# Merged tiles split into high and low parts inside the merging stage, whose block begins the output projection's first two tiles

## Chip, cores and metric

The kernel runs on one NeuronCore of a Trainium2 chip. The metric is the device time of one execution in microseconds (us); of the kernel before it is the median of three runs.

## The reference, cut to what matters

A block of four branches (RWKV-7, latent attention, convolution, memory attention) is run for two layers, and after it a second, different block. The change is in the end of each layer of the first block:

```
h = x @ w_in[l]                                   # x: 512 x 1024; merge: the last 4*1024 columns
branches = stack([y_rwkv, y_mla, y_conv, y_mem])  # 512 x 4 x 512
proj   = einsum('bsnc,ncd->bsnd', branches, w_o_branch[l])
gates  = sigmoid(merge.reshape(B, S, 4, D) + b_gate[l])
merged = sum(gates * proj, axis=2)                # 512 x 1024
out    = merged @ w_out[l]
x      = layer_norm(alpha * x + out)
```

Beside it the second block needs a modulation: silu(cond) (two rows of 1024) times a matrix w_ada of 1024 x 6144 in each of its two layers.

## The kernel before

Everything is kept transposed: a tile is 128 channels (partitions) by 512 positions, fp32, and a tensor of 1024 channels is eight tiles. A product of fp32 precision is made from three fp32r products: each operand is split into a high part (rounded by ScalarE's copy to fp32r) and a low part (what is left, by a subtraction). One output tile takes 24 matmuls: 8 of high weight x high data, 8 of high weight x low data (helper `with_high`, lines 155 and 158), 8 of low weight x high data.

**Weights** come as a stream of chunks of 512 KB (`Stream`, from line 93), each one a tile's weights of 1024 columns. SyncE sends chunk n into one of three ring slots, after the low part of chunk n-3 is made. ScalarE makes the high part (line 123) into one of two slots, after TensorE has begun the chunk before (count `used`), GpSimd makes the low part (line 131). All queues work strictly in the order written.

**The merging stage** of a layer is one block. A block ends on every engine when the slowest engine is done. It has 48 chunks, here counted 0 to 47. Step i (0 to 31) belongs to merged tile m = i // 4 and branch n = i % 4. TensorE takes them in pairs: the gate products of two steps (one chunk each, PSUM bank i % 4), then one chunk which holds w_o of both branches (PSUM banks 4 + n). So chunks 3p and 3p+1 are the gates of pair p and chunk 3p+2 is its projection. ScalarE takes the sigmoid of gate i (line 1669). VectorE first makes the low parts of the sixteen branch tiles (line 1682, count `branch_low`), then in step i multiplies product and gate (line 1690) and adds it to the merged tile in BR (line 1695).

**The modulation** is done by VectorE within the same steps (line 1703): w_ada comes as 48 rows of tiles ("rows", 512 KB each), and each row is multiplied and summed with the two conditions, two instructions a row. Row t is done in step i where 48 i // 30 <= t < 48 (i+1) // 30. SyncE issues rows and ring chunks from one queue, in turns: ahead of row t it sends the ring up to chunk 2 + 45 t // 48. Row t goes into one of four buffers, so row t (t >= 4) is issued when row t-4 is done (line 1630); rows 2 and 3 wait until the branch tiles that they overwrite are split (`branch_low` 12 and 16). The two conditions are loaded at the very start. After the last step a copy (line 1705) puts the modulation into `mods`.

**The output stage** (function `output`, line 1717) is the next block. ScalarE makes the high parts of the eight merged tiles and VectorE their low parts, and TensorE's tile t = 0 follows these k by k; tiles 1 to 7 have all eight. GpSimd goes on with low parts of weights. Then the residual is added. In layer 1 this block also loads parameters, constants and the context tile `ctxT` of the second block (`Context.sync`, lines 1896 to 1899), the last of these after `merged_low` 4, as it overwrites the merged tiles in BR, and normalises the context beside the products. SyncE begins a block by clearing 47 semaphores.

Of the kernel before, what the change touches and what calls it, by code (L numbers as in the profile page):

```python
# [174 lines left out]
def build(nc, A):  # L175
    with ExitStack() as ctx:
# [32 lines left out]
        with ExitStack() as one:  # L209
            first(nc, one, A, PS, XH, XL, BR, stream, mods, stage, loaded)  # L210
        with ExitStack() as two:
            second(nc, two, A, PS, XH, XL, BR, stream, mods, stage, constants, stored)
# [271 lines left out]
def first(nc, ctx, A, PS, XH, XL, BR, stream, mods, stage, loaded):  # L484
# [169 lines left out]
    for layer in range(LAYERS):  # L654
# [945 lines left out]
        Y = room.enter_context(nc.sbuf_tensor(f"merging{layer}", [P, 18 * T], F32))  # L1600

        def YT(i, n=1):
            return Y[:, i * T:(i + n) * T] if n == 1 else Y[:, i * T:(i + n) * T].rearrange("p (n t) -> p n t", n=n)

        GATE, WEIGHTED, MG = YT(0, 4), YT(4, 4), BR[:, 0:8, :]
        AD = WEIGHTED[:, 0, 0:96].rearrange("p (m c) -> p m c", c=2)
        PROD, CB = Y[:, 8 * T:10 * T], Y[:, 10 * T:14 * T].rearrange("p (c k) -> p c k", c=2)

# [3 lines left out]
        def rows_of(t):  # L1612
            s = t % 4
            return Y[:, (14 + 2 * s) * T:(16 + 2 * s) * T] if s < 2 else BR[:, 4 + 2 * s:6 + 2 * s, :].rearrange("p a t -> p (a t)")

        S, other = stage()
        with nc.Block() as block:
            @block.sync
            def _(sp):
                for c in range(2):  # L1620
                    sp.dma_start(CB[:, c, :], A["cond"][c].partition_broadcast(P)).then_inc(S("cond"), 16)
                stream.send(sp, n0 + RING)
                clear(sp, other)
                for t in range(48):
                    stream.send(sp, n0 + RING + 45 * t // 48)
                    if t >= 4:
                        sp.wait_ge(S("ada"), 2 * (t - 3))
                    elif t >= 2:
                        sp.wait_ge(S("branch_low"), 4 + 4 * t)
                    sp.dma_start(rows_of(t), A["ada"][layer, t, :, :]).then_inc(S(f"rows{t % 4}"), 16)  # L1630
                stream.send(sp, n0 + 48 + RING - 1)

            @block.tensor
            def _(pe):
                for m in range(8):
                    for n in (0, 2):
# [15 lines left out]
                        for nn in (n, n + 1):  # L1652
                            for k in range(4):
                                mm = nc.tensor.matmul(PS[:, 4 + nn, :], tile_of(stream.low(o), 4 * (nn % 2) + k), BH[:, 4 * nn + k, :], start=False, stop=(k == 3))
                            mm.then_inc(S("product"), 1)

            @block.scalar
            def _(act):
                def branch_high(b):
                    nc.scalar.activation(BH[:, b, :], BR[:, b, :], ACT.Copy).then_inc(S("branch_high"), 1)  # L1660

                stream.hi(nc, act, gate_chunk(1) + 1)
                for b in range(8):
                    branch_high(b)
                for i in range(32):
                    act.wait_ge(S("gate_product"), i + 1)
                    if i >= 4:
                        act.wait_ge(S("weighted"), i - 3)
                    nc.scalar.activation(GATE[:, i % 4, :], PS[:, i % 4, :], ACT.Sigmoid, bias=par_col("b_gate", 8 * (i % 4) + i // 4)).then_inc(S("gate"), 1)  # L1669
                    stream.hi(nc, act, min(gate_chunk(i) + (4 if i % 2 else 3), n0 + 48 + 1))  # L1670
                    if i == 0:
                        for b in range(8, 16):
                            branch_high(b)
                        act.wait_ge(S("cond"), 32)
                        nc.scalar.activation(CB, CB, ACT.Silu).then_inc(S("silu_c"), 1)

            @block.vector
            def _(dve):
# [4 lines left out]
                for i in range(32):  # L1683
# [3 lines left out]
                    dst = MG[:, m, :] if n == 0 else WEIGHTED[:, n, :]  # L1687
                    if i >= 4 and n:
                        dve.wait_ge(S("merged"), 3 * m - 3 + n)
                    v.tensor_tensor(dst, PS[:, 4 + i % 4, :], GATE[:, i % 4, :], ALU.mult).then_inc(S("weighted"), 1)  # L1690
                    if n:
                        dve.wait_ge(S("weighted"), i + 1)
                        if n > 1:
                            dve.wait_ge(S("merged"), 3 * m + n - 1)
                        v.tensor_tensor(MG[:, m, :], MG[:, m, :], WEIGHTED[:, n, :], ALU.add).then_inc(S("merged"), 1)
                    if i == 0:
                        dve.wait_ge(S("silu_c"), 1)
                    for t in range(min(48, 48 * i // 30), min(48, 48 * (i + 1) // 30)):
                        dve.wait_ge(S(f"rows{t % 4}"), 16 * (t // 4 + 1))
# [4 lines left out]
                dve.wait_ge(S("ada"), 96)  # L1704
                v.tensor_copy(mods[:, layer, :], WEIGHTED[:, 0, 0:96]).then_inc(S("mods"), 1)
# [7 lines left out]
        if layer == 0:  # L1713
            output(nc, PS, XH, XL, BR, stream, stage, base + FIRST["out"], layer, oneless[:, 0:1], C("ones"))


def output(nc, PS, XH, XL, BR, stream, stage, n0, layer, spare, ones, context=None):
# [4 lines left out]
    room = ExitStack()  # L1722
    MH, ML = (room.enter_context(nc.sbuf_tensor(f"merged_{part}{layer}", [P, DK, T], F32R))[:, :, :] for part in ("high", "low"))
    MG, RR, RUN = BR[:, 0:8, :], BR[:, 8:16, :], BR[:, 7, :]
    S, other = stage()
    with nc.Block() as block:
# [13 lines left out]
        def _(pe):  # L1740
            for t in range(8):
                if t >= 4:
                    pe.wait_ge(S("residual"), t - 3)
                if t == 0:
                    stream.wait_high(pe, n0)
                    for k in range(DK):
                        pe.wait_ge(S("merged_low"), k + 1)
                        with_high(nc, PS[:, 0, :], tile_of(stream.high(n0), k), MH[:, k, :], ML[:, k, :], k == 0, stream.used if k == 0 else None)
                    stream.wait_split(pe, n0)
                    for k in range(DK):  # L1750
                        mm = nc.tensor.matmul(PS[:, 0, :], tile_of(stream.low(n0), k), MH[:, k, :], start=False, stop=(k == DK - 1))
# [13 lines left out]
        def _(act):  # L1765
            a = nc.scalar
            for k in range(DK):
# [17 lines left out]
        def _(dve):  # L1785
            v = nc.vector
            for k in range(DK):
                dve.wait_ge(S("merged_high"), k + 1)
                v.tensor_tensor(ML[:, k, :], MG[:, k, :], MH[:, k, :].bitcast(F32), ALU.subtract).then_inc(S("merged_low"), 1)
            for t in range(8):  # L1790
# [4 lines left out]
                if t:  # L1795
# [3 lines left out]
                    if t == 1:  # L1799
                        dve.wait_ge(S("merged_low"), 8)  # L1800
# [3 lines left out]
    room.close()  # L1804
# [36 lines left out]
def second(nc, ctx, A, PS, XH, XL, BR, stream, mods, stage, constants, stored):  # L1841
# [44 lines left out]
    class Context:  # L1886
# [139 lines left out]
    for layer in range(LAYERS):  # L2026
# [7 lines left out]
        if layer == 0:  # L2034
            context = Context(mixed)
            output(nc, PS, XH, XL, BR, stream, stage, (LAYERS - 1) * NCHUNK1 + FIRST["out"], LAYERS - 1, spare[:, 0:1], C("ones"), context)
# [977 lines left out]
```

## Time and profile before

| | us |
|---|---|
| median of three runs | 3420.7 (3420.3 to 3421.48) |
| the profiled execution, its time | 3420.07 |
| its span, first to last instruction | 3418.3 |
| TensorE busy | 3225.6, 94% of the span |
| merging stage, layer 0, about | 597 to 868 |
| output stage, layer 0, about | 868 to 923 |

The span is what the profiler sees between the first and the last instruction; 1.8 us lie around it. Busy matmul time overlaps from one matmul to the next, so the distance from start to start is what a matmul costs. SPq is SyncE's DMA queue: a row of it is the time of issue, not of landing. The bracket at the end of a timeline row gives how long the engine was idle ahead of it and who released it.

### The profile page before, as it was taken

What the parts mean: (1) busy time and instruction counts of PE and PEld (TensorE: products, weight loads), DVE (VectorE), ACT (ScalarE), POOL (GpSimd) and SP (SyncE); (2) the same over time, 40 slices, a digit from 0 to 9 for tenths busy, and PEclk for the clock granted to TensorE, in tenths of its full rate; (3) what the DMA queues carried; (4) which work ended last, traced back from release to release, by engine and by line L of the source; (5) the groups of instructions that cost most, each with busy time, mean ns of one, the idle gap of its engine ahead of it and who ended that gap; (6) DMA issues with size and microseconds to landing.
All of it is one profiled execution on the core that took longest, in us unless ns stands there. A gap on an engine that the chain in (4) does not pass through costs nothing. (4 is left out here: it accounts for less than half of the span.)

```text
span 3418.3 us, 51762 instructions
## 1 busy us (share of the span) xinstructions
PE 3225.6 (94%) x21116; PEld 2532.1 (74%) x21116; DVE 1500.7 (44%) x2378; ACT 1188.0 (35%) x1940; POOL 1488.2 (44%) x820
## 2 busy tenths in 40 slices
PE   8899998999898999989998988999999989899999
PEld 6784786788577747867886756888888876678787
DVE  6633374898666333848896236210000022520000
ACT  6234433422362334343223435322112233532221
POOL 4431553454344225534552258333334433845454
PEclk9999999999999999999999999999999999999999
DMA  3011121555210111325552210212111111023232
GB/s 127 9 34 55 56 99 62 209 191 200 76 62 3 39 55 51 106 86 189 200 185 85 87 32 2 68 62 62 62 62 62 62 60 56 1 87 99 93 99 93
DMA packets 77611, 284.18 MB, mean 83 GB/s; under 512 B 8736, under 2 KB 8736, under 8 KB 76864
## 3 DMA queue, kind: packets, MB, share of 16 engines
q1 hardware_dynamic: 77376, 280.88, 24.4%
q8 instruction: 168, 2.75, 0.3%
q14 instruction: 67, 0.55, 0.1%
HBM read 278.75 MB, written 2.10 MB: 82 GB/s over the span
## 5 line engine op out<-in xcount | busy, mean ns | idle before, releaser
L131 POOL TENSOR_TENSOR lows<-ring,highs 128x1024 fp32r<-128x1024 f32 x376 | 939.1, 2498 | 1607.3 <-ACT highs L123 1590.4
L155 PE MATMUL ps<-x_high,highs 128*128 128x512 f32 x1936 | 771.6, 399 | 36.2 <-ACT highs L123 17.4
L158 PE MATMUL ps<-x_low,highs 128*128 128x512 f32 x1936 | 758.7, 392 | 0.0
L123 ACT ACTIVATE highs<-ring 128x1024 fp32r<-128x1024 f32 x376 | 396.9, 1056 | 749.9 <-PE ps L155 388.4
L155 PEld LDWEIGHTS ps<-x_high,highs 128*128 128x128 f32 x1936 | 366.2, 189 | 127.1 <-issue 30.7
L158 PEld LDWEIGHTS ps<-x_low,highs 128*128 128x128 f32 x1936 | 365.9, 189 | 78.3 <-issue 3.5
L2744 DVE TENSOR_TENSOR hidden_scratch<-ps,hidden_scratch 128x512 f32<-128x512 f32 x44 | 30.4, 692 | 546.0 <-PE ps L2063 541.5
L677 PE MATMUL ps<-x_high,lows 128*128 128x512 f32 x1040 | 256.8, 389 | 0.0
L677 PEld LDWEIGHTS ps<-x_high,lows 128*128 128x128 f32 x1040 | 195.3, 188 | 40.5
L2620 DVE SCALAR_TENSOR_TENSOR BR<-ps,mod,BR 128x512 f32<-128x512 f32 x72 | 47.4, 662 | 368.8 <-PE ps L167 368.8
L167 PE MATMUL ps<-hidden_parts,lows 128*128 128x512 f32 (+1 forms) x528 | 188.8, 358 | 0.0
L163 PE MATMUL ps<-hidden_parts,highs 128*128 128x512 f32 (+1 forms) x528 | 188.8, 358 | 0.0
L166 PE MATMUL ps<-hidden_parts,highs 128*128 128x512 f32 (+1 forms) x528 | 188.8, 358 | 0.0
L1703 DVE CUSTOM_DVE_ANT_0 merging<-merging 128x1024 f32<-128x1024 f32 x96 | 174.8, 1821 | 3.4
L2063 PE MATMUL ps<-x_high,lows 128*128 128x512 f32 x672 | 167.1, 391 | 0.0
L1703 DVE CUSTOM_DVE_ANT_0 merging<-BR,merging 128x1024 f32<-128x1024 f32 x96 | 164.3, 1711 | 5.5 <-DVE merging L1703 0.5
L428 POOL TENSOR_SCALAR tiles<-tiles 128x768 f32<-128x768 f32 (+1 forms) x80 | 154.9, 1948 | 25.5 <-DVE tiles L453 25.5
L1558 DVE SCALAR_TENSOR_TENSOR ps<-X,par,ps 128x512 f32<-128x512 f32 x232 | 152.9, 750 | 0.0
L2063 PEld LDWEIGHTS ps<-x_high,lows 128*128 128x128 f32 x672 | 123.3, 188 | 24.0
L428 POOL TENSOR_SCALAR X<-X 128x256 f32<-128x256 f32 (+3 forms) x96 | 97.7, 1032 | 67.2 <-DVE X L453 67.1
L1669 ACT ACTIVATE merging<-ps,par 128x512 f32<-128x512 f32 x64 | 44.1, 690 | 232.7 <-PE ps L677 232.7
L447 DVE TENSOR_REDUCE tiles<-ps 128x1 f32<-128x768 f32 (+1 forms) x80 | 67.7, 846 | 106.4 <-PE ps L330 106.2
(435 smaller groups left out, 5917.5 us busy)
## 6 DMA issues: line engine op xcount, KB each, us to landing
ring<-in_w SPq DMA_DIRECT2D x414, 512.0 KB, 3.5
merging<-in_ada SPq DMA_DIRECT2D x48, 512.0 KB, 3.5
BR<-in_ada SPq DMA_DIRECT2D x48, 512.0 KB, 3.5
X<-in_xT SPq DMA_DIRECT2D x4, 512.0 KB, 6.7
X<-in_memT SPq DMA_DIRECT2D x2, 1024.0 KB, 5.3
merging<-in_cond SPq DMA_DIRECT2D x4, 512.0 KB, 4.7
out<-BR SPq DMA_DIRECT2D x8, 256.0 KB, 4.4
cst<-in_cst SPq DMA_DIRECT2D x1, 1408.0 KB, 7.7
```

The lines of the kernel that those rows point to most:

```text
L123: nc.scalar.activation(self.high(n), self.chunk(n), ACT.Copy).then_inc(self.hi_made, 1)
L131: nc.gpsimd.tensor_tensor(self.low(n), self.chunk(n), self.high(n).bitcast(F32), ALU.subtract).then_inc(self.lo_made, 1)
L155: mm = nc.tensor.matmul(ps, high, xhigh, start=start, stop=False)
L158: nc.tensor.matmul(ps, high, xlow, start=False, stop=False)
L163: mm = nc.tensor.matmul(ps, high, xhigh, start=start, stop=False)
L166: nc.tensor.matmul(ps, high, xlow, start=False, stop=False)
L167: return nc.tensor.matmul(ps, low, xhigh, start=False, stop=stop)
L428: nc.gpsimd.tensor_scalar(prob(i, u), prob(i, u), stats[:, 3, n:n + 1], None, ALU.mult).then_inc(S("normed"), 1)
L677: mm = nc.tensor.matmul(PS[:, bank, :], tile_of(stream.low(n), k), xh[:, k, :], start=False, stop=(k == DK - 1))
L1558: ins = v.scalar_tensor_tensor(out=ACC[:, c, :] if tap == TAPS - 1 else acc, in0=H0[:, c, tap:tap + T], scalar=w, in1=acc, op0=ALU.mult, o ...
L1703: v.tensor_tensor_reduce(PROD, rows_of(t), CB[:, c, :], 1.0, 0.0, ALU.mult, ALU.add, AD[:, t, c:c + 1]).then_inc(S("ada"), 1)
L2063: mm = nc.tensor.matmul(ps, tile_of(stream.low(n), k), high[:, k, :], start=False, stop=(k == DK - 1))
```

## The change

- The merged tile is accumulated in one of two buffers in BR (tiles 8 and 9) instead of eight. In step i = 4m (m >= 1) ScalarE makes the high part of merged tile m-1, in step 4m+1 VectorE makes its low part, into tiles MH and ML that outlive the merging block. Only tile 7 is split in the output block.
- At the end of the merging block TensorE does the high-weight products of output tiles 0 and 1 for k = 0 to 6 (28 matmuls). The output block does k = 7 of each and its 8 low-weight products. ScalarE makes one more high part (chunk 49) in the merging block.
- Buffers: the gates have three buffers instead of four, the weighted product one instead of three, and both lie in BR with the conditions, the product scratch and two of the rows. So they wait for `branch_low`. The rows have three buffers instead of four: row t waits for row t-3. Row 0 has its own buffer; row 1 waits for `branch_low` 14, row 2 for 16; the conditions are loaded after `branch_low` 4, and SyncE clears the semaphores ahead of that.
- Row t is done in the step with 48 i // 29 <= t < 48 (i+1) // 29. The modulation is summed directly in `mods`; the copy at the end is gone. The wait of the context's load for `merged_low` 4 is gone.

```diff
-        Y = room.enter_context(nc.sbuf_tensor(f"merging{layer}", [P, 18 * T], F32))
-
-        def YT(i, n=1):
-            return Y[:, i * T:(i + n) * T] if n == 1 else Y[:, i * T:(i + n) * T].rearrange("p (n t) -> p n t", n=n)
-
-        GATE, WEIGHTED, MG = YT(0, 4), YT(4, 4), BR[:, 0:8, :]
-        AD = WEIGHTED[:, 0, 0:96].rearrange("p (m c) -> p m c", c=2)
-        PROD, CB = Y[:, 8 * T:10 * T], Y[:, 10 * T:14 * T].rearrange("p (c k) -> p c k", c=2)
+        Y = room.enter_context(nc.sbuf_tensor(f"merging{layer}", [P, 2 * T], F32))
+        kept = ExitStack()
+        MH, ML = (kept.enter_context(nc.sbuf_tensor(f"merged_{part}{layer}", [P, DK, T], F32R, side="right"))[:, :, :] for part in ("high", "low"))
+
+        def flat(a, n):
+            return BR[:, a:a + n, :].rearrange("p a t -> p (a t)")
+
+        CB, GATE, WEIGHTED = flat(0, 4).rearrange("p (c k) -> p c k", c=2), BR[:, 4:7, :], BR[:, 7, :]
+        MG, PROD = BR[:, 8:10, :], flat(10, 2)
+        AD = mods[:, layer, :].rearrange("p (m c) -> p m c", c=2)
+        ROWS = (Y[:, :], flat(12, 2), flat(14, 2))
...
+            return ROWS[t % 3]
 
         S, other = stage()
         with nc.Block() as block:
             @block.sync
             def _(sp):
+                stream.send(sp, n0 + RING)
+                clear(sp, other)
+                sp.dma_start(rows_of(0), A["ada"][layer, 0, :, :]).then_inc(S("rows0"), 16)
+                sp.wait_ge(S("branch_low"), 4)
                 for c in range(2):
                     sp.dma_start(CB[:, c, :], A["cond"][c].partition_broadcast(P)).then_inc(S("cond"), 16)
-                stream.send(sp, n0 + RING)
-                clear(sp, other)
-                for t in range(48):
+                for t in range(1, 48):
                     stream.send(sp, n0 + RING + 45 * t // 48)
-                    if t >= 4:
-                        sp.wait_ge(S("ada"), 2 * (t - 3))
-                    elif t >= 2:
-                        sp.wait_ge(S("branch_low"), 4 + 4 * t)
-                    sp.dma_start(rows_of(t), A["ada"][layer, t, :, :]).then_inc(S(f"rows{t % 4}"), 16)
+                    if t < 3:
+                        sp.wait_ge(S("branch_low"), 12 + 2 * t)
+                    else:
+                        sp.wait_ge(S("ada"), 2 * (t - 2))
+                    sp.dma_start(rows_of(t), A["ada"][layer, t, :, :]).then_inc(S(f"rows{t % 3}"), 16)
                 stream.send(sp, n0 + 48 + RING - 1)
...
+                for t in range(2):
+                    pe.wait_ge(S("gate"), 29 + t)
+                    stream.wait_high(pe, n0 + 48 + t)
+                    for k in range(7):
+                        pe.wait_ge(S("merged_low"), k + 1)
+                        with_high(nc, PS[:, t, :], tile_of(stream.high(n0 + 48 + t), k), MH[:, k, :], ML[:, k, :], k == 0, used if t == 0 and k == 0 else None)
...
-                    if i >= 4:
-                        act.wait_ge(S("weighted"), i - 3)
-                    nc.scalar.activation(GATE[:, i % 4, :], PS[:, i % 4, :], ACT.Sigmoid, bias=par_col("b_gate", 8 * (i % 4) + i // 4)).then_inc(S("gate"), 1)
+                    if i >= 3:
+                        act.wait_ge(S("weighted"), i - 2)
+                    else:
+                        act.wait_ge(S("branch_low"), 5 + i)
+                    nc.scalar.activation(GATE[:, i % 3, :], PS[:, i % 4, :], ACT.Sigmoid, bias=par_col("b_gate", 8 * (i % 4) + i // 4)).then_inc(S("gate"), 1)
                     stream.hi(nc, act, min(gate_chunk(i) + (4 if i % 2 else 3), n0 + 48 + 1))
+                    if i >= 4 and i % 4 == 0:
+                        act.wait_ge(S("merged"), 3 * i // 4)
+                        nc.scalar.activation(MH[:, i // 4 - 1, :], MG[:, (i // 4 - 1) % 2, :], ACT.Copy).then_inc(S("merged_high"), 1)
                     if i == 0:
                         for b in range(8, 16):
                             branch_high(b)
                         act.wait_ge(S("cond"), 32)
                         nc.scalar.activation(CB, CB, ACT.Silu).then_inc(S("silu_c"), 1)
+                stream.hi(nc, act, n0 + 48 + 2)
...
-                    dst = MG[:, m, :] if n == 0 else WEIGHTED[:, n, :]
-                    if i >= 4 and n:
-                        dve.wait_ge(S("merged"), 3 * m - 3 + n)
-                    v.tensor_tensor(dst, PS[:, 4 + i % 4, :], GATE[:, i % 4, :], ALU.mult).then_inc(S("weighted"), 1)
+                    if i == 0:
+                        dve.wait_ge(S("branch_low"), 16)
+                    if n:
+                        dve.wait_ge(S("merged"), 3 * m + n - 1)
+                    v.tensor_tensor(WEIGHTED if n else MG[:, m % 2, :], PS[:, 4 + i % 4, :], GATE[:, i % 3, :], ALU.mult).then_inc(S("weighted"), 1)
                     if n:
                         dve.wait_ge(S("weighted"), i + 1)
-                        if n > 1:
-                            dve.wait_ge(S("merged"), 3 * m + n - 1)
-                        v.tensor_tensor(MG[:, m, :], MG[:, m, :], WEIGHTED[:, n, :], ALU.add).then_inc(S("merged"), 1)
+                        v.tensor_tensor(MG[:, m % 2, :], MG[:, m % 2, :], WEIGHTED, ALU.add).then_inc(S("merged"), 1)
                     if i == 0:
                         dve.wait_ge(S("silu_c"), 1)
-                    for t in range(min(48, 48 * i // 30), min(48, 48 * (i + 1) // 30)):
-                        dve.wait_ge(S(f"rows{t % 4}"), 16 * (t // 4 + 1))
+                    if i >= 5 and n == 1:
+                        dve.wait_ge(S("merged_high"), m)
+                        v.tensor_tensor(ML[:, m - 1, :], MG[:, (m - 1) % 2, :], MH[:, m - 1, :].bitcast(F32), ALU.subtract).then_inc(S("merged_low"), 1)
+                    for t in range(min(48, 48 * i // 29), min(48, 48 * (i + 1) // 29)):
+                        dve.wait_ge(S(f"rows{t % 3}"), 16 * (t // 3 + 1))
                         for c in range(2):
                             if 2 * t + c:
                                 dve.wait_ge(S("ada"), 2 * t + c)
                             v.tensor_tensor_reduce(PROD, rows_of(t), CB[:, c, :], 1.0, 0.0, ALU.mult, ALU.add, AD[:, t, c:c + 1]).then_inc(S("ada"), 1)
-                dve.wait_ge(S("ada"), 96)
-                v.tensor_copy(mods[:, layer, :], WEIGHTED[:, 0, 0:96]).then_inc(S("mods"), 1)
...
-                if t == 0:
-                    stream.wait_high(pe, n0)
+                if t < 2:
+                    pe.wait_ge(S("merged_low"), 1)
+                    with_high(nc, PS[:, t, :], tile_of(stream.high(n0 + t), 7), MH[:, 7, :], ML[:, 7, :], False, stream.used if t else None)
+                    stream.wait_split(pe, n0 + t)
                     for k in range(DK):
-                        pe.wait_ge(S("merged_low"), k + 1)
-                        with_high(nc, PS[:, 0, :], tile_of(stream.high(n0), k), MH[:, k, :], ML[:, k, :], k == 0, stream.used if k == 0 else None)
-                    stream.wait_split(pe, n0)
-                    for k in range(DK):
-                        mm = nc.tensor.matmul(PS[:, 0, :], tile_of(stream.low(n0), k), MH[:, k, :], start=False, stop=(k == DK - 1))
+                        mm = nc.tensor.matmul(PS[:, t, :], tile_of(stream.low(n0 + t), k), MH[:, k, :], start=False, stop=(k == DK - 1))
...
-                a.activation(MH[:, k, :], MG[:, k, :], ACT.Copy).then_inc(S("merged_high"), 1)
-                if k == 1:
-                    stream.hi(nc, act, n0 + 2)
+            a.activation(MH[:, 7, :], BR[:, 9, :], ACT.Copy).then_inc(S("merged_high"), 1)
...
+            dve.wait_ge(S("merged_high"), 1)
+            v.tensor_tensor(ML[:, 7, :], BR[:, 9, :], MH[:, 7, :].bitcast(F32), ALU.subtract).then_inc(S("merged_low"), 1)
...
-            sp.wait_ge(S("merged_low"), 4)
             sp.dma_start(cT.rearrange("p k t -> p (k t)"), A["ctxT"]).then_inc(S("c_in"), 16)
```

## Rows read from the trace of the kernel before

**Rows 1.** The page's first part: busy us of each engine, its share, instructions.

```profile
PE 3225.6 (94%) x21116; PEld 2532.1 (74%) x21116; DVE 1500.7 (44%) x2378; ACT 1188.0 (35%) x1940; POOL 1488.2 (44%) x820
```

**Rows 2.** Busy by stretch: PE, PEld, DVE, ACT, POOL; clock, DMA, GB/s.

```profile
620.00:700.00 80.00, 80.00 (x350) 65.41 (x349) 66.63 (x75) 20.78 (x25) 38.39 (x15) 1.00 0.52 184
...
868.00:885.00 17.00, 12.25 (x40) 9.31 (x41) 8.15 (x11) 6.39 (x10) 4.35 (x2) 0.70 0.28 93
```

**Rows 3.** Timeline, end of merging, layer 0: start, us, engine, line, what.

```profile
862.33 2.03 PE L1654 MATMUL ps<-branches_high,lows 128*128 128x512 f32 x8
...
867.84 0.20 DVE L1705 COPY mods<-merging 128x96 f32<-128x96 f32 x1
...
868.34 1.15 ACT L1768 ACTIVATE merged_high<-BR 128x512 fp32r<-128x512 f32 x2 [7.92 <-PEq L1617]
...
869.85 0.76 PE L155 MATMUL ps<-merged_high,highs 128*128 128x512 f32 x1 [5.49 <-DVE merged_low L1789]
...
874.79 0.80 PE L155 MATMUL ps<-merged_high,highs 128*128 128x512 f32 x1 [2.90 <-DVE merged_low L1789]
...
881.36 0.40 PE L155 MATMUL ps<-merged_high,highs 128*128 128x512 f32 x1
...
886.96 0.40 PE L155 MATMUL ps<-merged_high,highs 128*128 128x512 f32 x1
```

**Rows 4.** Timeline of TensorE at the same place of layer 1.

```profile
1794.29 2.03 PE L1654 MATMUL ps<-branches_high,lows 128*128 128x512 f32 x8
...
1813.29 0.40 PE L155 MATMUL ps<-merged_high,highs 128*128 128x512 f32 x1
```

**Rows 5.** Timeline of SyncE's queue, start of merging, layer 0.

```profile
602.16 0.43 SPq L112 DMA_DIRECT2D ring<-in_w  x1
...
610.60 0.33 SPq L1630 DMA_DIRECT2D BR<-in_ada  x1
...
613.01 0.33 SPq L1630 DMA_DIRECT2D BR<-in_ada  x1
```

**Rows 6.** Timeline, ScalarE and TensorE: high of chunk 3, its use.

```profile
615.02 1.05 ACT L123 ACTIVATE highs<-ring 128x1024 fp32r<-128x1024 f32 x1
...
616.12 0.50 PE L155 MATMUL ps<-x_high,highs 128*128 128x512 f32 x1 [2.05 <-ACT highs L123]
```

**Rows 7.** Timeline of SyncE's queue: ring chunks 10, 19 and 33 before.

```profile
644.17 0.43 SPq L112 DMA_DIRECT2D ring<-in_w  x1
...
695.48 0.43 SPq L112 DMA_DIRECT2D ring<-in_w  x1
...
773.27 0.43 SPq L112 DMA_DIRECT2D ring<-in_w  x1
```

**Rows 8.** Timeline: TensorE's first of chunks 9, 18, 33; ScalarE's high of 19.

```profile
649.27 0.40 PE L155 MATMUL ps<-x_high,highs 128*128 128x512 f32 x1
...
698.87 0.40 PE L155 MATMUL ps<-x_high,highs 128*128 128x512 f32 x1
...
699.95 1.06 ACT L123 ACTIVATE highs<-ring 128x1024 fp32r<-128x1024 f32 x1 [4.35 <-DMA ring<-in_w]
...
781.53 0.40 PE L155 MATMUL ps<-x_high,highs 128*128 128x512 f32 x1
```

**Rows 9.** Stretch 600 to 868: low parts by form; line 1695, min/median/max ns.

```profile
L131 POOL TENSOR_TENSOR lows<-ring,highs 128x1024 fp32r<-128x1024 f32 x48 | 131.7, 2745 | 137.6 <-ACT highs L123 137.6
...
L1695 DVE TENSOR_TENSOR BR<-BR,merging x24: 691/695/2670, 617.0 to 867.2; 128x512 f32<-128x512 f32 x24
```

**Rows 10.** Timeline of TensorE after a wait elsewhere in the kernel.

```profile
2135.41 0.77 PE L163 MATMUL ps<-mixed_parts,highs 128*128 128x512 f32 x1 [2.49 <-DVE mixed_parts L2616]
...
2138.43 0.40 PE L166 MATMUL ps<-mixed_parts,highs 128*128 128x512 f32 x1
```

**Rows 11.** Output stage, layer 1: SyncE's first load; the context's DMA.

```profile
1803.71 0.33 SPq L1896 DMA_DIRECT2D par<-in_par  x1
...
BR<-in_ctxT SPq DMA_DIRECT2D x1, 1024.0 KB, 4.8
```

More of the change, by code:

```diff
@@ L209, in build @@
         with ExitStack() as one:
-            first(nc, one, A, PS, XH, XL, BR, stream, mods, stage, loaded)
+            merged = first(nc, one, A, PS, XH, XL, BR, stream, mods, stage, loaded)
         with ExitStack() as two:
-            second(nc, two, A, PS, XH, XL, BR, stream, mods, stage, constants, stored)
+            second(nc, two, A, PS, XH, XL, BR, stream, mods, stage, constants, stored, merged)
 def clear(sp, sems, done=None):
@@ L1612, in rows_of @@
         def rows_of(t):
-            s = t % 4
-            return Y[:, (14 + 2 * s) * T:(16 + 2 * s) * T] if s < 2 else BR[:, 4 + 2 * s:6 + 2 * s, :].rearrange("p a t -> p (a t)")
+            return ROWS[t % 3]
         S, other = stage()
@@ L1713, in first, with output @@
         if layer == 0:
[L1714 to L1724, printed above, removed]
+            output(nc, PS, XH, XL, BR, stream, stage, base + FIRST["out"], layer, oneless[:, 0:1], C("ones"), (kept, MH, ML))
+    return kept, MH, ML
+def output(nc, PS, XH, XL, BR, stream, stage, n0, layer, spare, ones, merged, context=None):
+    kept, MH, ML = merged
+    RR, RUN = BR[:, 8:16, :], BR[:, 7, :]
     S, other = stage()
@@ L1766, in _ @@
             a = nc.scalar
-            for k in range(DK):
-                a.activation(MH[:, k, :], MG[:, k, :], ACT.Copy).then_inc(S("merged_high"), 1)
-                if k == 1:
-                    stream.hi(nc, act, n0 + 2)
+            a.activation(MH[:, 7, :], BR[:, 9, :], ACT.Copy).then_inc(S("merged_high"), 1)
             for t in range(3, 10):
@@ L1786, in _ @@
             v = nc.vector
-            for k in range(DK):
-                dve.wait_ge(S("merged_high"), k + 1)
-                v.tensor_tensor(ML[:, k, :], MG[:, k, :], MH[:, k, :].bitcast(F32), ALU.subtract).then_inc(S("merged_low"), 1)
+            dve.wait_ge(S("merged_high"), 1)
+            v.tensor_tensor(ML[:, 7, :], BR[:, 9, :], MH[:, 7, :].bitcast(F32), ALU.subtract).then_inc(S("merged_low"), 1)
             for t in range(8):
@@ L1798, in _ @@
                         dve.wait_ge(S("run"), t - 1)
-                    if t == 1:
-                        dve.wait_ge(S("merged_low"), 8)
                     v.tensor_tensor(RUN, RR[:, 0, :] if t == 1 else RUN, RR[:, t, :], ALU.add).then_inc(S("run"), 1)
@@ L1803, in _ @@
                     context.vector(dve, S, t)
-    room.close()
+    kept.close()
 CKV = CTX + T
@@ L1838, with second @@
 NCHUNKS = _at
-def second(nc, ctx, A, PS, XH, XL, BR, stream, mods, stage, constants, stored):
+def second(nc, ctx, A, PS, XH, XL, BR, stream, mods, stage, constants, stored, merged):
     def sb(name, shape, dt=F32):
@@ L2035, in second @@
             context = Context(mixed)
-            output(nc, PS, XH, XL, BR, stream, stage, (LAYERS - 1) * NCHUNK1 + FIRST["out"], LAYERS - 1, spare[:, 0:1], C("ones"), context)
+            output(nc, PS, XH, XL, BR, stream, stage, (LAYERS - 1) * NCHUNK1 + FIRST["out"], LAYERS - 1, spare[:, 0:1], C("ones"), merged, context)
         lower = ExitStack()
```

## The prediction

> **What bounds the kernel now.** The page's first part comes first: the reader sees TensorE busy for 94% of the span and every other engine below half [rows 1]. So the time is TensorE's instructions plus what it waits, and a change which removes no matmul can only gain or lose waits. The stretches tell where they are: inside the merging stage TensorE has no idle time (80.00 of 80.00) at a granted clock of 1.00, while VectorE is busy for 66.63 of 80 us; from 868 to 885 TensorE is busy for 12.25 of 17.00 us, and the clock is 0.70, partly at its lower level of 1.2 GHz [rows 2]. The timeline of that place shows why: the last projection matmuls of merging start at 862.33, VectorE ends with the modulation's copy at 868.04, ScalarE's first high part starts 0.30 us later, and TensorE's first matmul of the output at 869.85, after 5.49 us of idleness; a second wait of 2.90 us follows at 874.79 [rows 3]. Layer 1 repeats it: 19.00 us from its last group to the first matmul of output tile 1, against 19.03 in layer 0 [rows 3, 4]. Last I read SyncE's queue in merging, since the change shortens its lookahead [rows 5, 7].
>
> **The junction: what goes.** I count from Z, the start of the last group of eight projection matmuls. Matmuls at full clock start (886.96 - 881.36) / 24 = 0.233 us apart. Before, output tile 2 starts at Z + 24.63 (886.96 - 862.33) in layer 0 and at Z + 19.00 + 5.60 = Z + 24.60 in layer 1. After, the group of eight takes 1.87, then 28 matmuls 6.53, and the last is done at about Z + 8.56. VectorE is no longer the last to end the block: it ended at Z + 5.71 with the copy of 0.20, and its rows now end one step sooner, so TensorE ends it. The low part of merged tile 6 is made in step 29, before the last products are out, and covers nothing more. Then 0.30 for the next block and 1.51 (868.34 to 869.85) for high and low part of tile 7: TensorE goes on at Z + 10.37. Twenty matmuls (k = 7 twice for each of two tiles, eight low ones for each) take 4.67: tile 2 starts at Z + 15.04. That is 9.59 us less in layer 0 and 9.56 in layer 1, **19.15 in all**. The idle time there falls to 1.8 us. What is late next is ScalarE's high part of chunk 50: it waits for tile 1's first matmul of this block, ten matmuls after Z + 10.37, so it is made by about Z + 14.2, under a microsecond ahead of tile 2.
>
> **The clock at the junction.** A wait of 2.05 us left the following matmuls 0.4 us long [rows 6]; one of 2.49 was followed by 0.77, and seven start-to-start distances took 3.02 us where full clock needs 1.63 [rows 10]. 1.8 us is below the first, so I take nothing; if it falls after all, it costs 1.4 a layer. I keep 0 to 2.8 for the range.
>
> **The start of merging: chunk 3.** Ring and rows share one queue, in order. Before, chunk 3 was sent at 602.16, ahead of row 2's wait. After, row 1 stands ahead of it and waits for `branch_low` 14. The counts 12 and 16 came by 610.60 and 613.01 [rows 5], so 14 by about 611.8, and chunk 3 is sent at 612.2. A chunk behind a row took 4.47 us from issue (695.48) to ScalarE's start on it (699.95) [rows 7, 8], and from that start to TensorE's first matmul it is 1.10 (615.02 to 616.12) [rows 6]: 617.8, **1.6 us later** than 616.12. The wait there grows from 2.05 to 3.7 us, over the 2.49 that was followed by the lower clock, so 1.4 more [rows 10]. A landing 1 us faster or slower, my bounds for a transfer that here meets others, makes the delay 0.6 to 2.6. The gates' new waits for `branch_low` 5 to 7 and the later conditions (sent at `branch_low` 4, used after ScalarE's sixteen branch splits) hide behind those splits, in which `branch_low` goes from 4 to 12 and beyond; the covers are over once a landing takes longer than from `branch_low` 4 to ScalarE's last split.
>
> **Three row buffers: later ring chunks.** Row t waits for row t-3 instead of t-4, and VectorE's rows until step 7 are nearly the same, so a chunk of the first half is sent when its successor was before. Chunk 9 goes at chunk 10's time, 644.17 [rows 7]: 644.17 + 4.47 + 1.10 = 649.74 against TensorE's start on it at 649.27 [rows 8]: **0.5**. Chunk 18 goes at chunk 19's time, 695.48: 701.05 against 698.87, 2.2 late; VectorE has one new subtraction ahead of row 14 in step 9, 0.69 us by the like-sized addition of line 1695 (its longest, beside GpSimd, is 2.67 [rows 9]): **2.9**. That wait too is over 2.49: 1.4 more for the clock. The delays add up, since VectorE starts each pair of steps by waiting for TensorE's products and moves with it. In the second half the tighter spread (29 instead of 30) has VectorE one row ahead: row 30 moves from step 19 to 18, takes row 29's place, and chunk 33 goes at 773.27 as before, needed at 781.53, after 773.27 + 5.57 = 778.84 [rows 7, 8]. Nothing more is late there. Together a layer loses 1.6 + 0.5 + 2.9 + 2 x 1.4 = 7.8, **15.6 in all**. Bounds of the layer's loss: 0.6 (only chunk 3, fast landing, clock kept) to 13 (2.6 + 0.5 + 4.9 + 2.8, and 2 for chunks with under a microsecond to spare).
>
> **VectorE and GpSimd.** Seven subtractions of 0.69 are added a layer, ScalarE gets seven copies, and the copy to `mods` goes. Each lies beside TensorE's 80.00 of 80.00; VectorE has 13 us idle in such 80 [rows 2]. But line 1695, 0.695 in the median, takes up to 2.67, by about the length of one GpSimd low part (131.7 / 48 = 2.74) [rows 9]: the two engines exclude each other in part. The sum above takes no cost from it. The Trainium skill, page "SBUF — State Buffer", section "Who interferes with whom", says that a VectorE operation with two SBUF inputs and a GpSimd operation that reads SBUF hold the shared port pair in turns, the later one blocked until the first is done. By that rule the added subtractions and the denser rows would also hold up GpSimd; that is the third case below. The trace agrees as far as 0.69 against 2.67 shows it.
>
> **Layer 1's output stage.** SyncE's par load was issued at 1803.71, about 3.4 us after its block began (1794.29 + 6.01) [rows 4, 11]. After, that is Z + 12.3, the context (1024 KB, 4.8 us to landing [rows 11]) at Z + 13.1, and chunk 51 behind it lands at Z + 19.4 to 20.9 (estimate: half and up to the whole of 3 us more than the context's 17.9). Tile 3 starts at Z + 15.04 + 5.60 = 20.64 and needs it 1.10 before: 0 to 1.4 late. I take 0.7. The wait for `merged_low` 4 is replaced by the later start of the block.
>
> **Sum.** Profiled execution 3420.07 - 19.15 + 15.6 + 0.7 = 3417.2; the median of the runs is 0.6 above that execution: **3418**.
>
> **Rivals.** (a) Forecast: the junction's gain is given back in merging by late ring chunks. For it: chunk 19 already waited on its landing [rows 8], and there is one buffer less. Against it: TensorE never waited there before. 3418, own range 3413 to 3427; chance 0.50.
> (b) The later sends stay hidden (chunks land faster, or VectorE's rows come early enough), and only chunk 3 is late, 1.6 and 1.4 a layer: 3420.7 - 19.15 + 6.0 = 3407.5. For it: chunk 9's margin is half a microsecond, and 5.57 us from send to use may be less where nothing is queued ahead. Chance 0.28.
> (c) Slower: VectorE and GpSimd become the bound of merging. In a pair of steps (16.5 us: 698.87 - 649.27 is three of them) GpSimd makes three low parts, 8.2 us, and VectorE now has 6.6 row instructions, 1.5 additions, 2 products and half a subtraction. In 80 us it was busy 66.63; 3.4% more rows and 0.35 a pair make 70.5, and each blocking lengthens one of the two. It decides once VectorE no longer waits for TensorE at the start of a pair: then rows slip, chunks too, by some 0.35 us a pair over fifteen pairs, 5 a layer more than in (a): 3418 + 10 = 3428 to 3431. Against it: 13 us idle in 80. Chance 0.19.
> (d) The early matmuls don't run ahead of the block's end, because the low part of tile 6 or chunk 49 is late: the gain falls to about 3 a layer, and the time to 3431. Against it: step 29 lies a whole projection chunk ahead of the end. Chance 0.03.
>
> **Numbers.** About 0.2% (6.8 us) is what a measurement of this kernel can tell from no change, so faster is below 3413.9 and slower above 3427.5. Faster: (b) and a little of (a), 0.31. Slower: (c), (d) less the cases that end under it, 0.20. Same: 0.49. The range 3406 to 3430 takes in (b), (a) and most of (c), with the clock at the junction inside.
>
> **What would show it.** Right: TensorE's idle time ahead of the first output-block matmul near 1.8 us at full clock, and tile 2 at Z + 15; chunk 3 sent near 612 and used near 618, with the lower clock behind it; TensorE waiting for ScalarE's highs at chunk 18, which wait for the ring's landing. Wrong: no TensorE waits between 620 and 868 (then b), VectorE never idle there and TensorE waiting at many chunks (then c), or matmuls of 0.63 us after the junction.

## The result and the profile after

The changed kernel takes 3428.47 us (median of 20 runs, 3423.81 to 3433.35), the kernel before 3420.8 (20 runs beside them). The ratio is 1.0021 with a 95% interval of 1.0015 to 1.0028: slower by 7 to 8 us, where 3418 and "no change" were forecast. The range, 3406 to 3430, holds the time; the direction was not the one with the highest chance (slower had 0.20), and the point is 10.5 us off. The profiled execution spans 3426.3 us, 8.0 more than before.

The page's first part and three stretches of the changed kernel (columns as in rows 2). TensorE has as much to do as in [rows 1], and now it has idle time inside merging, where [rows 2] had none:

```profile
PE 3229.0 (94%) x21116; PEld 2532.0 (74%) x21116; DVE 1516.8 (44%) x2376; ACT 1190.1 (35%) x1940; POOL 1487.2 (43%) x820
...
620.00:700.00 80.00, 78.87 (x334) 63.63 (x335) 61.34 (x68) 21.55 (x26) 39.49 (x15) 0.98 0.51 185
700.00:780.00 80.00, 77.73 (x332) 63.02 (x331) 73.73 (x80) 21.67 (x25) 39.53 (x14) 0.98 0.53 189
...
878.00:890.00 12.00, 8.78 (x32) 6.67 (x31) 3.08 (x3) 0.77 (x2) 2.34 (x1) 0.87 0.31 110
```

The junction of layer 0 in the changed kernel's timeline, which answers to [rows 3]:

```profile
874.72 2.03 PE L1658 MATMUL ps<-branches_high,lows 128*128 128x512 f32 x8
...
882.89 0.39 PE L158 MATMUL ps<-merged_low,highs 128*128 128x512 f32 x1
...
883.56 0.63 ACT L1781 ACTIVATE merged_high<-BR 128x512 fp32r<-128x512 f32 x1 [5.42 <-PEq L1619]
883.56 2.34 POOL L131 TENSOR_TENSOR lows<-ring,highs 128x1024 fp32r<-128x1024 f32 x1 [8.27 <-POOLq L1619]
884.22 2.23 DVE L1799 TENSOR_TENSOR merged_low<-BR,merged_high 128x512 fp32r<-128x512 f32 x1 [5.34 <-ACT merged_high L1781]
...
886.51 0.57 PE L155 MATMUL ps<-merged_high,highs 128*128 128x512 f32 x1 [3.23 <-DVE merged_low L1799]
886.88 0.63 PE L158 MATMUL ps<-merged_low,highs 128*128 128x512 f32 x1
887.30 3.35 PE L1765 MATMUL ps<-merged_high,lows 128*128 128x512 f32 x8
...
892.82 0.40 PE L155 MATMUL ps<-merged_high,highs 128*128 128x512 f32 x1
```

The 28 early matmuls run without a gap, the first from 876.59, the last from 882.89. Then GpSimd begins the low part of chunk 49 in the same instant in which the output block begins, and VectorE's low part of tile 7, beside it, takes 2.23 us instead of 0.69. TensorE waits 3.23 us, and most of the next matmuls are 0.63 us long instead of 0.40, at the lower level of 1.2 GHz. Tile 2 starts 18.10 us after the last group of eight (892.82 - 874.72), where before it was 24.63.

The start of merging, answering to [rows 5, 6] (SyncE's queue, ScalarE, TensorE):

```profile
605.23 1.28 ACT L1681 ACT_TABLE_LOAD   x1 [1.37 <-DVE branches_low L1698]
...
614.24 0.33 SPq L1634 DMA_DIRECT2D BR<-in_ada  x1
614.61 0.43 SPq L112 DMA_DIRECT2D ring<-in_w  x1
...
619.07 1.06 ACT L123 ACTIVATE highs<-ring 128x1024 fp32r<-128x1024 f32 x1 [1.51 <-DMA ring<-in_w]
...
620.18 0.50 PE L155 MATMUL ps<-x_high,highs 128*128 128x512 f32 x1 [4.80 <-ACT highs L123]
620.51 0.59 PE L158 MATMUL ps<-x_low,highs 128*128 128x512 f32 x1
620.90 0.63 PE L155 MATMUL ps<-x_high,highs 128*128 128x512 f32 x1
```

ScalarE's first gate needs a table load (1.28 us), and its wait for `branch_low` 5 holds that load back too. Row 1 goes at 614.24, chunk 3 behind it, and ScalarE waits for it to land; TensorE starts on it at 620.18, after 4.80 us of idleness, and the lower clock follows. Chunk 18, answering to [rows 7, 8]:

```profile
703.00 0.43 SPq L112 DMA_DIRECT2D ring<-in_w  x1
...
707.43 1.06 ACT L123 ACTIVATE highs<-ring 128x1024 fp32r<-128x1024 f32 x1 [5.95 <-DMA ring<-in_w]
...
708.63 0.48 PE L155 MATMUL ps<-x_high,highs 128*128 128x512 f32 x1 [2.27 <-ACT highs L123]
```

What TensorE waited for from 597 to 895 (columns: us, times, longest), in the changed kernel:

```profile
PE ps L155 <- ACT highs L123: 8.7, 5, 4.8
PE ps L155 <- DVE merged_low L1799: 3.2, 1, 3.2
```

From the timeline I read the starts of all 48 chunks of both layers. A stage's loss is the distance from chunk 0 to chunk 47 less that of the kernel before; a term is the place where this difference jumps. The junction's gain is found the same way, from the distance between chunk 47 and output tile 2, which was 28.37 us before.

| us | layer 0 | layer 1 | predicted, per layer |
|---|---|---|---|
| chunk 3 late | 2.8 | 2.9 | 1.6 |
| lower clock in chunk 3 | 1.6 | 1.6 | 1.4 |
| chunks 8 to 15 late | 1.7 | 1.5 | 0.5 |
| chunk 18 late, with the clock behind it | 4.1 | 1.4 | 4.3 |
| chunk 33 late | 0.9 | 1.1 | 0 |
| stage, sum | 11.1 | 8.6 | 7.8 |
| junction, gain | 6.5 | 6.7 | 9.6 |
| tile 3 waits for chunk 51 | | 1.5 | 0.7 |

The sum is 19.7 - 13.2 + 1.5 = 8.0, against 8.0 between the spans. The stages ahead of merging, which the change does not touch, were 1.3 us longer ahead of layer 0 and 1.5 shorter ahead of layer 1 than in the execution before, and nearly cancel here. The runs of one kernel scatter by some microseconds (3423.8 to 3433.4 for the changed one), and each has a profile of one execution only. So the places below are read from profiles; the times say whether the sum is right, and where a profiled execution lies well off its kernel's median, that is said.

### The profile page after: what moved, and what is told of

Its sections match the earlier page's. It is cut to its first block and busy times, and to the rows that moved or that the text cites. A ratio compares the mean times of both kernels' runs of the same rounds, so it can differ in the third digit from the quotient of the medians.

```text
span 3426.3 us, 51736 instructions
## 1 busy us (share of the span) xinstructions
PE 3229.0 (94%) x21116; PEld 2532.0 (74%) x21116; DVE 1516.8 (44%) x2376; ACT 1190.1 (35%) x1940; POOL 1487.2 (43%) x820
## 5 line engine op out<-in xcount | busy, mean ns | idle before, releaser
L1721 DVE CUSTOM_DVE_ANT_0 BR<-BR 128x1024 f32<-128x1024 f32 x128 | 229.6, 1794 | 6.0
L1721 DVE CUSTOM_DVE_ANT_0 BR<-merging,BR 128x1024 f32<-128x1024 f32 x64 | 142.2, 2221 | 2.8
L166 PEld LDWEIGHTS ps<-hidden_parts,highs 128*128 128x128 f32 x528 | 99.4, 188 | 16.1
```

The costliest lines, as they stand in the source:

```text
L166: nc.tensor.matmul(ps, high, xlow, start=False, stop=False)
L1721: v.tensor_tensor_reduce(PROD, rows_of(t), CB[:, c, :], 1.0, 0.0, ALU.mult, ALU.add, AD[:, t, c:c + 1]).then_inc(S("ada"), 1)
```

## The experiments

**Chunk 3 ahead of row 1.**

```diff
-                    stream.send(sp, n0 + RING + 45 * t // 48)
+                    stream.send(sp, n0 + RING + max(1, 45 * t // 48))
```

> The changed kernel with one difference: ring chunk 3 is sent ahead of row 1's wait for branch_low 14, not behind it. Theory (late ring chunks): chunk 3 lands long before ScalarE is free for it (its gate of step 1 ends at 617.56 in the changed kernel's trace), so TensorE starts on it 1.5 us earlier; the wait stays above 3 us and the lower clock behind it stays. Two layers: 3.0 us less than the changed kernel, some 3425.5. Rival (VectorE and GpSimd bound merging): the later waits at chunks 18 and 33 grow by as much, and nothing is gained, 3428.5.

3425.0 us (ratio to before 1.0007, 0.9999 to 1.0016). Chunk 3 is issued at 605.99, ScalarE no longer waits for it, and TensorE starts on it 18.81 + 1.13 us after chunk 0, 1.6 us sooner than in the changed kernel. The jump at chunk 3 falls from 2.8 and 2.9 to 1.1 and 1.3; those at 8 to 33 stay in the main. The clock was misjudged for the profiled execution: the wait of 3.18 us left the matmuls behind it at 0.40 us, their length at full clock, so 1.6 more went in each layer. That execution took 3421.95, which is 3 us under the median; the median fits the expected 3425.5, in which the clock does fall. How often it falls in the other runs, no profile shows.

```profile
619.12 0.50 PE L155 MATMUL ps<-x_high,highs 128*128 128x512 f32 x1 [3.18 <-ACT highs L123]
619.46 0.40 PE L158 MATMUL ps<-x_low,highs 128*128 128x512 f32 x1
```

**Four row buffers.**

```diff
-        Y = room.enter_context(nc.sbuf_tensor(f"merging{layer}", [P, 2 * T], F32))
+        Y = room.enter_context(nc.sbuf_tensor(f"merging{layer}", [P, 4 * T], F32))
...
-        ROWS = (Y[:, :], flat(12, 2), flat(14, 2))
+        ROWS = (Y[:, 0:2 * T], flat(12, 2), flat(14, 2), Y[:, 2 * T:4 * T])
...
-                    else:
-                        sp.wait_ge(S("ada"), 2 * (t - 2))
+                    elif t >= 4:
+                        sp.wait_ge(S("ada"), 2 * (t - 3))
...
+    MH7, ML7 = (last.enter_context(nc.sbuf_tensor(f"last_{part}{layer}", [P, T], F32R))[:, :] for part in ("high", "low"))
```

> The changed kernel with four row buffers again instead of three (row t waits for row t-4; the space comes from tile 7's high and low parts, which become tensors of the output block). Everything else of the change stays. Theory (three row buffers make ring chunks late): TensorE's waits at chunks 8 to 18 and 33 go, with the lower clock behind 18: 0.83 + 4.12 + 0.87 us in layer 0, 1.5 + 1.5 + 1.2 in layer 1, about 10 us less than the changed kernel, some 3418.5. Rival (the seven subtractions and the denser rows load the port that VectorE and GpSimd share): the waits stay, 3427 to 3429.

3419.97 us (0.9994, 0.9986 to 1.0003). The stage's loss is 4.7 and 4.5 us, all of it at chunks 3 and 4; no jump is left at 8, 9, 11, 14, 18 or 33, in either layer. TensorE's waits from 597 to 900:

```profile
PE ps L155 <- ACT highs L123: 5.1, 1, 5.1
PE ps L155 <- DVE last_low L1808: 3.2, 1, 3.2
```

One wait for ScalarE where the changed kernel had five: the missing buffer makes the others.

**The first gates in tiles that are split first.**

```diff
-        CB, GATE, WEIGHTED = flat(0, 4).rearrange("p (c k) -> p c k", c=2), BR[:, 4:7, :], BR[:, 7, :]
+        CB, GATE, WEIGHTED = flat(4, 4).rearrange("p (c k) -> p c k", c=2), BR[:, 0:3, :], BR[:, 3, :]
...
-                sp.wait_ge(S("branch_low"), 4)
+                sp.wait_ge(S("branch_low"), 8)
...
-                        act.wait_ge(S("branch_low"), 5 + i)
+                        act.wait_ge(S("branch_low"), 1 + i)
```

> The changed kernel with gates and conditions changing places in BR: the first gates wait for branch_low 1 to 3 instead of 5 to 7, the conditions' load for 8 instead of 4. Theory (the gate's wait puts off ScalarE's table load by 1.3 us and with it branch splits 9 to 16, branch_low 14, row 1 and chunk 3): TensorE starts on chunk 3 1.3 us earlier, 2.6 us for two layers, some 3426. Rival (only the queue order counts, ScalarE's delay is hidden): no difference, 3428.5; if the conditions, issued 3.7 us later, land after ScalarE's last split, it is slower.

3424.71 us (1.0008, 0.9999 to 1.0017). The jump at chunk 3 is 1.5 and 1.6 instead of 2.8 and 2.9. ScalarE's table load starts with no wait ahead of it, and row 1 and chunk 3 follow 1.3 us sooner:

```profile
601.65 1.28 ACT L1681 ACT_TABLE_LOAD   x1
...
616.66 0.50 PE L155 MATMUL ps<-x_high,highs 128*128 128x512 f32 x1 [3.54 <-ACT highs L123]
617.00 0.39 PE L158 MATMUL ps<-x_low,highs 128*128 128x512 f32 x1
```

The wait that I had hidden behind the branch splits costs 1.3 us a layer; what is left, 1.5 and 1.6, is the 1.6 that the prediction had for the order of the queue alone. Again the clock stayed up, after 3.54 us. This execution took 3419.45, the fastest of the eleven and 5 us under their median, so it does not stand for all of them as to the clock.

**Chunk 49's low part in the merging block.**

```diff
-                stream.lo(nc, pool, n0 + 48 + 1)
+                stream.lo(nc, pool, n0 + 48 + 2)
```

> The changed kernel with GpSimd's low part of chunk 49 made in the merging block, not at the start of the output block. Theory (that low part holds up VectorE's low part of tile 7, 2.23 us instead of 0.68, and the wait of 3.23 us then drops TensorE's clock): the wait falls to 1.7, matmuls behind it stay at 0.4 us, 1.55 + 1.65 = 3.2 us a layer, 6.4 in all, some 3422. Rival (the lower clock comes anyway): 3.1 us in all, 3425.4. Rival (ScalarE or SyncE end the wait, not VectorE): nothing.

3425.95 us (1.0012, 1.0003 to 1.0021). The junction does as expected in both layers: gain 9.6 and 9.6 instead of 6.5 and 6.7.

```profile
884.68 0.63 ACT L1781 ACTIVATE merged_high<-BR 128x512 fp32r<-128x512 f32 x1 [5.42 <-PEq L1619]
885.34 0.69 DVE L1799 TENSOR_TENSOR merged_low<-BR,merged_high 128x512 fp32r<-128x512 f32 x1 [5.34 <-ACT merged_high L1781]
886.09 0.50 PE L155 MATMUL ps<-merged_high,highs 128*128 128x512 f32 x1 [1.69 <-DVE merged_low L1799]
...
886.66 2.02 PE L1765 MATMUL ps<-merged_high,lows 128*128 128x512 f32 x8
```

VectorE's 2.23 is 0.69 again, the wait 1.69, and eight matmuls take 2.02 us instead of 3.35. The median fell by 2.5 only, not by 6.4, to the time of the rival "the lower clock comes anyway"; its reason is refuted by the rows, as the clock stays up. In the profiled execution layer 1's stage lost 10.8 (3.3 at chunk 18 and 1.7 for the lower clock behind it, where the changed kernel's profile had 1.4), and tile 3 waited 1.9. Whether that is scatter or a consequence of the mend was not separated.

**The kernel before with three row buffers.**

```diff
-            s = t % 4
+            s = t % 3
...
-                    if t >= 4:
-                        sp.wait_ge(S("ada"), 2 * (t - 3))
+                    if t >= 3:
+                        sp.wait_ge(S("ada"), 2 * (t - 2))
```

> The kernel before with three row buffers instead of four and nothing else of the change. Theory (lookahead of the rows sets when ring chunks are sent): TensorE waits for late chunks with no part of the split in the stage. By before's own rows the sends move to the next chunk's time: about 0.5 at chunk 9, 2.2 at 18 and, as its rows keep the looser spread, 2 to 3 at 33, each of the long ones with up to 1.7 for the lower clock: 5 to 8 us a layer, 3431 to 3437. Rival (VectorE's added work makes rows late): no more than 1 us a layer, 3421 to 3423.

3440.06 us (1.0047, 1.0034 to 1.006), more than expected. The profiled stages lose 10.8 and 10.0 us: 2.8 and 2.9 at chunk 18, 3.1 and 3.0 at 33, 1.0 and 0.4 at 26, 0.9 at chunk 3 of layer 0, and the lower clock behind one of them in each layer (1.7 behind chunk 33, 3.0 behind chunk 18). TensorE's waits from 597 to 900:

```profile
PE ps L155 <- ACT highs L123: 9.6, 5, 3.0
PE ps L155 <- DVE merged_low L1789: 8.4, 2, 5.5
```

The late chunks come with no part of the split, the new layout or the early matmuls present. That is the loss of the missing buffer by itself, at the looser spread.

**No subtractions on VectorE.**

```diff
+                        nc.scalar.activation(ML[:, i // 4 - 1, :], MG[:, (i // 4 - 1) % 2, :], ACT.Copy).then_inc(S("merged_low"), 1)
...
-                    if i >= 5 and n == 1:
-                        dve.wait_ge(S("merged_high"), m)
-                        v.tensor_tensor(ML[:, m - 1, :], MG[:, (m - 1) % 2, :], MH[:, m - 1, :].bitcast(F32), ALU.subtract).then_inc(S("merged_low"), 1)
```

> The changed kernel with the seven low parts in the merging stage written by a copy of ScalarE instead of VectorE's subtraction, so VectorE has none of the split's work there (the low parts hold a copy of the merged tile, not the remainder: that part of the computation is changed). Theory (the subtractions cost at most their 0.69 us once, ahead of row 14): waits at chunks 3, 8 to 18 and 33 stay, 1 us a layer less at most, 3426 to 3428.5. Rival (the subtractions and GpSimd's low parts hold each other up): the waits at 8 to 33 go, 10 us less, near 3418.

3425.39 us (1.0008, 0.9999 to 1.0017), between the two. The waits stay: stages lose 8.4 and 7.6, chunk 18 is 1.9 and 1.5 late. What goes is small: 0.5 at chunk 18 of layer 0, 0.9 at its chunk 33, and the lower clock behind its chunk 18 (1.7). The stages lose 16.0 in all instead of 19.7, so the subtractions are a minor part: 2 us of waits in two layers, 3.7 with the clock, and 3.1 between the medians. That holds although the subtraction ahead of row 14 took 2.88 us in the changed kernel (at 697.30) and not the 0.69 of the prediction.

**Rows spread as before.**

```diff
-                    for t in range(min(48, 48 * i // 29), min(48, 48 * (i + 1) // 29)):
+                    for t in range(min(48, 48 * i // 30), min(48, 48 * (i + 1) // 30)):
```

> The changed kernel with the rows spread as before (48 i // 30) instead of 48 i // 29. Theory (the tighter spread lets VectorE be a row ahead in the second half and pays there for the missing buffer): chunk 33 and its like become 2 to 4 us late, 4 to 8 us more than the changed kernel over two layers, 3432 to 3436. Rival (denser rows only load VectorE and GpSimd's port): faster by some us, 3424 to 3427.

3446.24 us (1.0064, 1.0052 to 1.0077), even slower than expected. Chunk 33 is 3.1 and 3.4 us late instead of 0.9 and 1.1, chunk 44 1.0 in layer 0, chunk 26 1.2 in layer 1, and the lower clock follows chunk 33 of layer 1 (1.7); the stages lose 15.7 and 17.4. The denser spread is no load to speak of: it pays for most of the missing buffer in the second half. Chunk 18 was later too in this execution, 3.1 and 3.9 us instead of 2.4 and 1.4; why, was not separated.

**The four mends together.** The edits of ring_first, four_rows, gate_apart and low49 in one kernel.

> The changed kernel with the four mends of ring_first, four_rows, gate_apart and low49 together. Theory: the stage's loss falls to 0 to 0.5 us a layer (it was 11.1 and 8.6), the junction gives 9.6 a layer, 1.4 to 1.9 stay at layer 1's tile 3: 3421 - 19.2 + 1 + 1.9 = 3404 to 3406. Rival (mends overlap, as waits move on to the next late thing): 3408 to 3413.

3406.81 us (0.995, 0.9938 to 0.9963). Layer 0 loses nothing in the stage (-0.2 us), and its junction gains 9.6:

```profile
PE ps L155 <- ACT highs L123: 1.8, 1, 1.8
PE ps L155 <- DVE last_low L1808: 1.7, 1, 1.7
```

Layer 1 loses 1.7, as a wait at chunk 3 no longer than in the kernel before was followed by the lower clock in this execution. Its tile 3 waits 3.09 us for chunk 51, more than the 1.4 to 1.9 expected, with 1.6 more for the lower clock behind it; the chunk lands behind the context's loads:

```profile
1537.70 0.79 PE L155 MATMUL ps<-x_high,highs 128*128 128x512 f32 x1 [2.02 <-ACT highs L123]
1538.30 0.63 PE L158 MATMUL ps<-x_low,highs 128*128 128x512 f32 x1
...
1809.37 0.50 PE L155 MATMUL ps<-merged_high,highs 128*128 128x512 f32 x1 [3.09 <-ACT highs L123]
```

**And chunks 51 and 52 ahead of the context's loads.**

```diff
-            stream.send(sp, n0 + RING)
+            stream.send(sp, n0 + RING + 2)
             clear(sp, other)
```

> all_four with one difference: in the output block ring chunks 51 and 52 are sent ahead of the semaphore clearing and of layer 1's par, constant and context loads. Theory (in layer 1 chunk 51 lands behind 1.5 MB of those loads and makes TensorE wait 3.09 us at tile 3 in all_four's trace, with a slower stretch behind it): that wait goes, 3 to 4 us less than all_four, 3402 to 3404. Rival (the context's later landing moves the wait to its squares and the ring chunks behind them): nothing, 3406 to 3408.

3404.87 us (0.9957, 0.9943 to 0.9971). The wait at tile 3 is gone: tiles 2 and 3 of layer 1 start 18.77 and 24.38 us after chunk 47, 5.61 apart. The two stages lose -0.2 and 0.0 us. The queue, with the ring ahead of the loads:

```profile
1794.18 1.28 SPq L112 DMA_DIRECT2D ring<-in_w  x3
1798.64 0.33 SPq L1914 DMA_DIRECT2D par<-in_par  x1
```

Against all_four the intervals overlap, so the 2 us between them are shown by the profile's place, not by the time. By the ratio this version is 0.43% (14.7 us) faster than the kernel before, by the medians 16.5 us; its median is 23.6 under that of the changed kernel.

## Why the prediction was wrong

The mechanism was the one forecast, (a), and its places were named beforehand: chunk 3 behind row 1, chunk 18, which is sent once row 14 is done, and the junction. What failed is the sum. It had 2.9 us of gain in the profiled execution where 8.0 of loss were measured, 10.9 us apart: 5.9 at the junction, 2.5 at chunk 3 and 0.4 for the clock behind it, 4.2 at chunks 8 to 15 and 33, 0.8 at tile 3, and 3.1 the other way at chunk 18 (0.2 lies in jumps under 0.1). This last term was luck: without it the time would have come to some 3431.5, outside the range.

- **The junction: what goes** (9.59 and 9.56, measured 6.5 and 6.7) was the largest miss, 5.9 us over both layers. The arithmetic of the matmuls was right, as low49 shows (1.69 us of wait against 1.8, gain 9.6). What failed is the step "1.51 (868.34 to 869.85) for high and low part of tile 7", taken from rows in which GpSimd was idle. Before, ScalarE could make chunk 49's high part only after TensorE had begun output tile 0, and GpSimd's low part of it came behind that; after the change this high part is ready at the end of merging, so GpSimd's first instruction of the block is released in the same instant as ScalarE's and holds VectorE for 1.54 us. I had written down the blocking [rows 9] and applied it to the stage only. The step "I take nothing" for the clock at the junction fell with it: what is left of the miss, 1.5 us in layer 0 and 1.3 in layer 1, is the lower clock behind the wait of 3.2 us.
- **The start of merging: chunk 3** (1.6) measured 2.8 and 2.9. Landing was right (4.46 us from issue to ScalarE's start, 4.47 used). The step that failed is that the gates' new waits "hide behind those splits": the waiting gate stands in front of eight splits in ScalarE's queue, so `branch_low` 14 comes 1.3 us later (gate_apart, in which 1.5 and 1.6 are left).
- **Three row buffers** (0.5 + 2.9 + 1.4). At chunk 18 of layer 0 the size was near (2.4 and 1.7 for the clock), as far as one execution tells; in layer 1 the chunk was 1.4 us late and the clock stayed up, 2.9 us less than forecast. Three chunks with under a microsecond to spare (8, 11, 14) and chunk 33 were counted as in time; with the forecast 0.5 of chunk 9 these places measured 2.6 a layer. four_rows, in which they are all in time again, shows that the missing buffer makes them late; no_dve_low puts the part of VectorE's added subtractions at 2 us of waits in both layers, 3.7 with the clock, and how the rest divides was not separated.
- **Layer 1's output stage** (0.7) measured 1.5, next to its upper bound of 1.4, and that was luck too. The context's load, issued right behind two others, landed after 8.06 us instead of 4.8, and chunk 51 at Z + 23.9 where 19.4 to 20.9 was estimated (the 3 us in that estimate stand in no row); but the junction's shortfall had put tile 3 off by 3 us as well. With the junction mended the wait is 1.9 (low49) and 3.1 (all_four).
- Rival (c), the port as the bound of merging, gave a time near the measured one, 3428 to 3431, but not for its reason: four_rows keeps all the work on VectorE and GpSimd and is rid of every wait from chunk 8 to 33, and the denser spread is faster, not slower (spread30). Rivals (b) and (d) did not happen: chunks were late, and the early matmuls ran without a gap.

GpSimd had held VectorE in the same way in the kernel before, at merged tile 2, and some 1.7 us (2.42 - 0.69) of its wait of 2.90 at 874.79 [rows 3] came from it: GpSimd's low part of chunk 49 began 0.47 us ahead of VectorE's low part of that tile, which then took 2.42 us.

```profile
871.84 2.35 POOL L131 TENSOR_TENSOR lows<-ring,highs 128x1024 fp32r<-128x1024 f32 x1 [8.93 <-ACT highs L123]
872.31 2.42 DVE L1789 TENSOR_TENSOR merged_low<-BR,merged_high 128x512 fp32r<-128x512 f32 x1 [2.02 <-ACT merged_high L1768]
```

The prediction took this wait as gone with the split and did not ask what had made it.

The rule cited from the Trainium skill, page "SBUF — State Buffer", section "Who interferes with whom" (of a VectorE operation with two SBUF inputs and a GpSimd operation that reads SBUF, the later one waits for the other's end), was not used where it mattered. The trace agrees at the junction: VectorE's subtraction, begun 0.66 us after GpSimd's, ends when GpSimd's 2.34 us are over plus its own length (883.56 + 2.34 + 0.69 = 886.59, measured 886.45). By that rule, applied there, the junction's gain would have come to 8.0 a layer before any change of the clock.

## What to carry to other kernels

When work is moved ahead of a block's end, ask which other engine's first instruction it releases into the stretch that stays on the path. When a buffer is taken away, follow what shares its queue: here one row buffer less did no harm to the rows' own user, and delayed the weight chunks that are sent behind them. A wait on one instruction delays all that stand behind it in its queue, even where that instruction itself has time.

## What was not expected of the hardware

The length of a wait of 2 to 3.5 us did not tell whether the clock falls. In the prediction 2.05 us kept and 2.49 us lost it. In the runs the matmuls behind 3.18 and 3.54 us (chunk 3 of ring_first and gate_apart) stayed at 0.39 to 0.40 us, while 2.02 us (chunk 3 of layer 1 in all_four) was followed by 0.63 us matmuls and a chunk 1.57 us longer, and 2.27 us (chunk 18) cost 1.69. Nearly the same wait at the same place went either way: at chunk 3, 2.05 us in layer 0 of the kernel before kept the clock and 2.02 us in all_four lost it. So in this kernel such a wait is priced with a chance, not with a bound. The 3.2 us at the junction was followed by the lower clock in every profile that has it, and so were all waits of 4.7 us and more in merging and at the junction.

A VectorE subtraction of 128x512 with two SBUF inputs takes 0.69 us, and took 2.23 to 2.88 us where a low part of 128x1024 on GpSimd (2.34 to 2.57 us) had begun 0.2 to 0.7 us before it. At the start of a block, where both engines are released together, that length can lie on the path in full.
